# Delta rule of the RWKV-7 half: masked products and keys merged in their order of use, and one empty slot per tile left out

## The reference, cut to what matters

```python
def _rwkv7_scan(r, w, k, v, a, b, s0, reverse, emit):
    def step(s, inp):
        r_t, w_t, k_t, v_t, a_t, b_t = inp
        sa = jnp.einsum('bhvk,bhk->bhv', s, a_t)
        s = s * w_t[:, :, None, :] + sa[..., None] * b_t[:, :, None, :] + v_t[..., None] * k_t[:, :, None, :]
        y = jnp.einsum('bhvk,bhk->bhv', s, r_t) if emit else None
        return s, y
...
s_fin, ys = lax.scan(step, s0, xs, reverse=reverse)
...
y = ys[0] + ys[1]
mu = jnp.mean(y, axis=-1, keepdims=True)
var = jnp.mean(jnp.square(y - mu), axis=-1, keepdims=True)
yn = ((y - mu) * lax.rsqrt(var + RW_GN_EPS)).reshape(bsz, l, RW_WIDTH) * lnx_g + lnx_b
yn = yn + (bonus[0] + bonus[1]).reshape(bsz, l, RW_WIDTH)
```

## Time and profile before

| | us |
|---|---|
| median of 3 runs | 3844.43 (3835.66 to 3857.89) |
| profiled execution | 3846.75, its span 3844.9 |
| this stage, first load issued to last output normed | 772.90 to 1296.40, some 523 |
| PE busy over the span | 3337.7 (87%) |
| DVE, ACT, POOL busy over the span | 2382.1, 1908.6, 824.9 |

### The profile page before, as it was taken

One profiled execution on the slowest core, in us unless ns is written; L12 is line 12 of the kernel. 1 busy time (PEld: TensorE's weight loads), 2 busy tenths in 40 slices (PEclk: granted clock), 3 DMA queues, 4 the chain that ended last, 5 costly groups with the idle time before them and its releaser, 6 DMA issues. The chain is left out here.

```text
span 3844.9 us, 90156 instructions
## 1 busy us (share of the span) xinstructions
PE 3337.7 (87%) x33248; PEld 2259.3 (59%) x33248; DVE 2382.1 (62%) x4428; ACT 1908.6 (50%) x2994; POOL 824.9 (21%) x1095
## 2 busy tenths in 40 slices
PE   4899799768888697879989989999699999698699
PEld 0899798756666575633333333333377778576577
DVE  1688688845566575537767767777485753076631
ACT  0576567645555343217757767776423221066520
POOL 4000000045666200522212222221332323100000
PEclk6999899879999798989999999999999999898899
DMA  8354534432233337669799999950724223465352
GB/s 318 78 165 160 163 128 146 164 85 59 58 82 102 123 101 250 121 233 323 228 293 351 337 349 345 293 139 9 250 76 121 66 82 104 113 145 137 106 174 77
DMA packets 561734, 639.75 MB, mean 166 GB/s; under 512 B 108682, under 2 KB 472998, under 8 KB 558230
## 3 DMA queue, kind: packets, MB, share of 16 engines
q1 hardware_dynamic: 536038, 564.59, 46.2%
q0 software_dynamic: 25216, 69.34, 7.4%
q10 hardware_dynamic: 48, 0.05, 0.0%
HBM read 489.41 MB, written 161.74 MB: 169 GB/s over the span
## 5 line engine op out<-in xcount | busy, mean ns | idle before, releaser
L2626 PE MATMUL routed_p_gu<-routed_fixed,routed_x 128*32 128x512 f32 x3840 | 569.6, 597 | 0.0
L2626 PE MATMUL routed_p_gu<-moe_exp_w,routed_x 128*32 x1280 | 568.6, 597 | 0.7 <-DVE routed_fixed L2741 0.7
L2741 DVE COPY routed_fixed<-moe_exp_w 128x1024 f32 x640 | 400.5, 684 | 47.9 <-DMA moe_exp_w<-in_exp_w_up_dram 39.6
L2680 ACT COPY routed_fixed<-moe_exp_w 128x1024 f32 x320 | 332.7, 1047 | 148.2 <-PE routed_p_y L2641 78.1
L544 PE MATMUL front_ps<-front_a_high,front_w_high 128*128 128x320 f32 (+1 forms) x1120 | 363.3, 324 | 16.4 <-DVE front_w_low L797 13.5
L544 PE MATMUL front_ps<-front_a_high,front_w_low 128*128 128x320 f32 (+1 forms) x1120 | 354.4, 316 | 0.0
L544 PE MATMUL front_ps<-front_a_low,front_w_high 128*128 128x320 f32 (+1 forms) x1120 | 354.3, 316 | 0.0
L2626 PEld LDWEIGHTS routed_p_gu<-moe_exp_w,routed_x 128*32 128x32 f32 x1280 | 135.0, 110 | 353.8 <-issue 353.8
L2693 ACT COPY routed_fixed<-routed_wd 128x1024 f32 x240 | 235.3, 1043 | 127.2 <-PE routed_p_gu L2626 91.3
L3650 PE MATMUL pre_ps<-pre_a_high,pre_w_high 128*128 128x512 f32 x720 | 286.9, 399 | 13.2 <-ACT pre_xb L3811 6.6
L2641 PE MATMUL routed_p_y<-routed_wd,routed_hT 128*32 x640 | 289.1, 594 | 5.2 <-ACT routed_fixed L2693 5.2
(11 more groups left out here) (547 smaller groups left out, 7483.9 us busy)
## 6 DMA issues: line engine op xcount, KB each, us to landing
moe_exp_w<-in_exp_w_gate_dram SPq DMA_DIRECT2D x64, 1024.0 KB
moe_exp_w<-in_exp_w_up_dram SPq DMA_DIRECT2D x64, 1024.0 KB
routed_wd<-in_exp_w_down_dram SPq DMA_DIRECT2D x64, 1024.0 KB
front_wt<-in_w_in_dram SPq DMA_DIRECT2D x70, 512.0 KB, 4.4
mod_w<-in_w_mod_dram SPq DMA_DIRECT2D x24, 1024.0 KB, 18.2
pre_wt<-in_w_in_dram SPq DMA_DIRECT2D x44, 512.0 KB, 4.0
rw_abrk<-front_rb SPq DMA_DIRECT2D x64, 320.0 KB
rwmix_src<-rw_abrk SPq DMA_DIRECT2D x80, 192.0 KB, 2.5
```

The source lines that it names most:

```text
L2626: op = nc.tensor.matmul(p_gu[spot(s), :], x[:, b % 2, k, spot(s)], w, start=(k == 0), stop=(k == KD - 1))
L2680: nc.scalar.copy(fixed[:, place_of(b, c), 0, :], wgu[:, bass.ds(e % WS, 1), c * D:(c + 1) * D].rearrange("p o n -> p (o n)"))\
L2741: op = nc.vector.tensor_copy(fixed[:, place_of(b, c), s - 1, :], wgu[:, bass.ds(es[s] % WS, 1), c * D:(c + 1) * D].rearrange("p o n -> p ( ...
```

## The change

Three things are done at once. First, b leaves `src` and is loaded into a new tile `pair` in halves of 64 tokens, each beside the half of k that is used with it, so that a tile's b and k have one layout `[channel, d, step, token half]`: 14 DMAs per group and tile in place of 10. Second, the transposes of b and k write d = 0 into one bank and d = 1 into the other, in the layout of `bk`, and the products write their results by kind of product, not by chunk (`product_to`): each of the copies to `bk`, and each of the masks `at` and `bkT`, is then one instruction over 128 partitions in place of two over 64. Third, the slot `rest1` is left out of the list, so that `t0` stands two slots behind `prod`, and a tile has 23 slots (31 with the norm). `OFFSET` stays 6.

```diff
-    A, R, B, K, V = 0, 1, 2, 0, 1
+    A, R, V = 0, 1, 0
-        src, kv = each("src", [P, 2, 3, 2, P]), each("kv", [P, 2, 2, 2, P])
+        src, kv = each("src", [P, 2, 2, 2, P]), each("kv", [P, 2, 1, 2, P])
+        pair = each("pair", [P, 2, 2, 2, P])
-        LOADS = 10
+        LOADS = 14
-            out = ["turn", "lay", "rest0", "prod", "masked", "rest1", "t0"] + norm[0:1]
+            out = ["turn", "lay", "rest0", "prod", "masked", "t0"] + norm[0:1]
+        def product_to(b, rows, h, d, c, other):
+            first, last = 2 * other + d, 4 + 2 * c + d
+            return b[rows, h, :].rearrange("p (k t) -> p k t", t=HEAD)[:, slice(first, last + 1, last - first), :]
-                    sp.dma_start(src[u][:, z, :, d, :], rw["abrk"][d, 0:3, rows, tk].rearrange("j p t -> p j t"))\
+                    sp.dma_start(src[u][:, z, :, d, :], rw["abrk"][d, 0:2, rows, tk].rearrange("j p t -> p j t"))\
-                        sp.dma_start(kv[u][:, z, K, d, half(1 - c)], rw["k"][d, rows, tk]).then_inc(loaded[u][z], 16)
+                        at_step = chunk_of(c, d)
+                        sp.dma_start(pair[u][:, z, d, at_step, half(c)], rw["abrk"][d, 2, rows, tk]).then_inc(loaded[u][z], 16)
+                        sp.dma_start(pair[u][:, z, d, at_step, half(1 - c)], rw["k"][d, rows, tk]).then_inc(loaded[u][z], 16)
...
-                    for bank, first, rows in ((0, 0, x[:, B]), (0, 2 * P, kv[u][:, z, V]), (1, 0, kv[u][:, z, K])):
-                        for d in range(2):
-                            op = nc.tensor.transpose(b[:, bank, span(first + d * P, P)], rows[:, d], consts["ident"][:, :])
+                    for d in range(2):
+                        for s in range(2):
+                            nc.tensor.transpose(b[:, d, span(s * P, P)], pair[u][:, z, d, s], consts["ident"][:, :])
+                    for d in range(2):
+                        op = nc.tensor.transpose(b[:, 0, span(2 * P + d * P, P)], kv[u][:, z, V, d], consts["ident"][:, :])
...
-                    for side in range(2):
-                        op = nc.scalar.copy(stacked_rows(bk[u], side, side), turned_rows(b, 0, 0, side))
-                    op.then_inc(by_scalar[u], 1)
+                    nc.scalar.copy(bk[u][:, 0].rearrange("p s t -> p (s t)"), b[:, 0, span(0, 2 * P)]).then_inc(by_scalar[u], 1)
...
+                def product(k):
+                    return b[:, :, span(k * P, P)].rearrange("p h (e t) -> p h e t", e=2)
                 def strict(out, other):
-                    for c in range(2):
-                        rows = half(1 - c if other else c)
-                        op = nc.vector.tensor_tensor(out[u][rows].rearrange("p (e h) t -> p h e t", h=2), product(rows, c, 0),
-                                                     mask(MASK_AFTER)[rows].rearrange("p e h t -> p h e t"), ALU.mult)
-                    op.then_inc(by_vector[u], 1)
+                    nc.vector.tensor_tensor(out[u][:].rearrange("p (e h) t -> p h e t", h=2), product(other),
+                                            mask(MASK_AFTER).rearrange("p e h t -> p h e t"), ALU.mult).then_inc(by_vector[u], 1)
                 if p == "turn":
-                    for side in range(2):
-                        op = nc.vector.tensor_copy(stacked_rows(bk[u], side, 1 - side), turned_rows(b, 1, 0, side))
-                    op.then_inc(by_vector[u], 1)
+                    nc.vector.tensor_copy(bk[u][:, 1].rearrange("p s t -> p (s t)"), b[:, 1, span(0, 2 * P)]).then_inc(by_vector[u], 1)
```

More of the change, by code:

```diff
@@ L1196, in body @@
                             for h in range(2):
-                                to = span((2 * c + d) * P, P)
                                 queries = x[half(h), A:R + 1, d, half(c)]
-                                nc.tensor.matmul(b[half(c), h, to], x[half(h), B, d, half(c)], queries, start=True, stop=True)
-                                op = nc.tensor.matmul(b[half(1 - c), h, to], kv[u][half(h), z, K, d, half(1 - c)], queries,
+                                nc.tensor.matmul(product_to(b, half(c), h, d, c, 0), pair[u][half(h), z, d, chunk_of(c, d), half(c)], queries,
+                                                 start=True, stop=True)
+                                op = nc.tensor.matmul(product_to(b, half(1 - c), h, d, c, 1), pair[u][half(h), z, d, chunk_of(c, d), half(1 - c)], queries,
                                                       start=True, stop=True)
@@ L1349, in heads @@
                     return ap.rearrange("p h e v -> p (h e) v")
-                def product(rows, c, side):
-                    v = b[rows, :, span(2 * P * c, 2 * P)].rearrange("p h (e j t) -> p h e j t", e=2, j=2)
-                    return v[:, :, :, side, :]
+                def product(k):
+                    return b[:, :, span(k * P, P)].rearrange("p h (e t) -> p h e t", e=2)
                 def strict(out, other):
-                    for c in range(2):
-                        rows = half(1 - c if other else c)
-                        op = nc.vector.tensor_tensor(out[u][rows].rearrange("p (e h) t -> p h e t", h=2), product(rows, c, 0),
-                                                     mask(MASK_AFTER)[rows].rearrange("p e h t -> p h e t"), ALU.mult)
-                    op.then_inc(by_vector[u], 1)
+                    nc.vector.tensor_tensor(out[u][:].rearrange("p (e h) t -> p h e t", h=2), product(other),
+                                            mask(MASK_AFTER).rearrange("p e h t -> p h e t"), ALU.mult).then_inc(by_vector[u], 1)
                 if p == "turn":
                     PE.wait(dve, products[u], n, p)
-                    for side in range(2):
-                        op = nc.vector.tensor_copy(stacked_rows(bk[u], side, 1 - side), turned_rows(b, 1, 0, side))
-                    op.then_inc(by_vector[u], 1)
+                    nc.vector.tensor_copy(bk[u][:, 1].rearrange("p s t -> p (s t)"), b[:, 1, span(0, 2 * P)]).then_inc(by_vector[u], 1)
                 elif p == "prod":
@@ L1373, in body @@
                     for c in range(2):
-                        op = nc.vector.tensor_tensor(cc[u][:, c], product(slice(0, P), c, 1),
+                        op = nc.vector.tensor_tensor(cc[u][:, c], product(2 + c),
                                                      mask(MASK_FROM).rearrange("p e h t -> p h e t"), ALU.mult)
```

## The result

The change takes **3862.79 us** (median of 20 runs; one of them took 6703.07 and is left out of the ratio), the kernel before 3846.86 beside it: ratio **1.0033 [1.0024, 1.0042]**. That is slower, within the 0.5% that was forecast as no change, and 9 us over the 3854 predicted. The profiled execution took 3862.59.

The account below looks back on a forecast made before the run. The order of 24 steps was taken to bind, with no engine full. Plain tiles +12.6, normed tiles -5.1 and loads +1.7 make +9.2 on the profiled 3846.75, 3856; with the median 2.3 lower, 3854 us, range 3830 to 3878.

Parts of the forecast that it names:

- Loads: First tile: PE's first transpose stands behind fourteen DMA issues, not ten, +1.7 us; later loads stay ahead.
- Plain tiles: Tiles 0 to 6, without the norm: a period goes from 46.55 to 48.35 us, +1.8; seven of them +12.6.
- windows of 4.98: From a group's products to its `t0`: each window costs the DVE and POOL floor, 4.98 us; -3.2 per period.
- Gaps: From a group's `t0` to the next group's products: 7.4, 7.4, 9.1 and 4.5 us; +1.7 (first two), +2.7, +0.6.
- Third gap: Behind group 2's `t0`: S of group 0 waits for POOL's `faded`; 9.1 us for 6.40, +2.7; bounds 7.4 and 10.0.
- two waits of S per period: Sign in the changed profile: DVE's S waits for POOL's `faded` twice per period, 1.5 to 2 us.
- The merge's worth: Merging saves 1.27 us of DVE per group and tile, nearly all covered; one `at` piece lowers the window's floor to 4.98.
- DVE's relief reaches the path: Faster rival: 5.1 us of DVE work leave each period, plain period 43.8 us, total 3822; chance 0.12.
- Normed tiles: Three periods with the norm, 32 steps before: the whole left-out step is gained, -5.1 us; ends -5.1 and +5.4.
- The clock: Rival: more waiting on PE drops its clock to 1.2 GHz; one such period costs some 34 us, 3888; chance 0.04.

Follow-up runs that it names:

- the runs without the identity: POOL's identity addition on `TT` left out, in the change (ratio 0.9969) and in the change with slot `rest1` kept (0.9952); ratios to the kernel before.
- The merge alone: The change with slot `rest1` kept (24 steps), so merged instructions and new loads only; ratio 0.9960 to the kernel before.
- Masks later: The change with POOL's second and third X made one slot later, in the slot of `t0`; ratio 0.9993 to the kernel before.
- The run without the identity: The change with POOL's identity addition on `TT` left out; ratio 0.9969 to the kernel before.
- the best kernel: The change with `rest1` kept, `rest0` left out in tiles without the norm, both states' `faded` made early; ratio 0.9874 to the kernel before.
- other slot, state early: The change with `rest1` kept, `rest0` left out instead, and the first state's `faded` made in the slot of `t4`; ratio 0.9979 to the kernel before.

## Why the prediction held, and where its steps failed

- **Loads**: +1.7 forecast; +1.6 measured at PE's first transpose, +1.1 at the first products, counted from the first load. The first transpose (780.70) came 1.85 us behind the last of fourteen issues, 1.98 behind the last of ten before. The rule of the Trainium skill that transfers under 512 bytes don't reach line rate (DMA: Bandwidth & Descriptors, Specifications) shows no cost here: the eight loads into `pair` of the first tile landed 2.0 us behind their issue (median), where the four of k, with rows as short, took 2.2 before, and the two of `src` 2.2, where they took 2.4.

```profile
778.85 0.43 SPq L1145 DMA_DIRECT2D rwmix_kv<-rw_v  x1
...
780.70 1.12 PE L1197 MATMUL rwmix_ps<-ident,rwmix_pair 128*128 128x128 f32 x4 [31.21 <-DMA rwmix_kv<-rw_v]
```

- **Plain tiles**: +12.6 forecast, +13.0 measured, and the hit is in part luck. The working: windows of 4.98 hold in groups 1 to 3 and the runs without the identity show why; the windows' sum is 20.85 (forecast 19.9), since group 0's is 5.2 to 6.4. Gaps 7.14, 7.14, 8.5 to 9.2, 4.2 to 4.7 (forecast 7.4, 7.4, 9.1, 4.5) sum to 27.89, forecast 28.4. Where no low clock falls into them, the pieces are 5.18, three of 4.98, and 7.14, 7.14, 8.53, 4.24: a period of 47.2 and not 48.35. The gaps were forecast 1.35 us too long, and the clock, which had no term in the sum, made up for most of that.
- **Third gap**: two waits of S per period, as said, but of 3.0 us on the mean and not 1.5 to 2. The kernel before has two as well (13 in the same stretch, of 0.4 and 1.9 us in steady tiles), where the prediction read one; so their number was no sign of the change, their length was. The gap was priced at 1.7 us above the one with S on time (9.1 against 7.4); the runs put it at 0.9 (8.77 against 7.91) before S waits for PE instead. The rest of the 9.1 was PE's own chain.
- **The merge's worth** was put at one piece of `at` per window, 12 us of plain tiles. The merge alone gained 8.3 there and 6.6 in the normed tiles; beside the slot it is worth 29.7 (370.8 against 341.1). That fits the rival "DVE's relief reaches the path" for the merge; the slot took it back.
- **Normed tiles** are the step that failed, the term "I take the whole step, -5.1 us": -1.5 measured (+0.65, -1.57, -0.55 to the stage's end). The sum was 3.6 us short by this term. In tile 8 the windows lost 5.5 us together and the gaps gained 4.0, where none was taken for them; 1.8 of that is the last gap, 17.39 for 15.63 in tile 7, with the same work at a lower clock (by stretch, tile 7 and tile 8):

```profile
1164.00:1179.63 15.63, 12.74 (x375) 9.87 (x379) 8.32 (x26) 9.34 (x29) 9.24 (x18) 1.00 0.15 36
1215.46:1232.85 17.39, 14.97 (x374) 11.64 (x378) 8.26 (x26) 9.33 (x29) 9.26 (x18) 0.80 0.24 64
```

"Masks later" has the same order on PE and a clock of 1.00 in tiles 7 and 8, and is 3.8 us shorter there: 1.6 in group 0's window of tile 7 (5.18 for 6.78) and 2.0 in that last gap, while every other window and gap agrees within 0.3. So by this comparison most of what the term lacks is the clock, which it left out. The run without the identity is 7.3 us shorter in these two tiles, with windows 4.5 shorter than those of "masks later"; so POOL's row binds there as well.

- **The clock** was a rival at 0.04, priced for a whole period at the lower level. It came, but for some 4 us in each period (0.04 to 0.05 of 48 us are missing in the granted clock, and it has only a half to lose). Group 0's window in tiles 3 to 5 (the same work), and the time around its products in tile 5, by stretch:

```profile
931.11:936.28 5.17, 4.68 (x162) 3.96 (x158) 2.53 (x8) 3.04 (x10) 2.67 (x6) 1.00 0.03 6
978.75:985.14 6.39, 6.09 (x160) 5.14 (x158) 2.32 (x7) 2.83 (x9) 2.82 (x6) 0.76 0.02 4
1027.64:1033.80 6.16, 5.62 (x160) 4.90 (x158) 2.56 (x8) 3.01 (x9) 2.68 (x6) 0.84 0.01 3
...
1020.00:1026.00 6.00, 3.20 (x78) 2.38 (x77) 2.33 (x8) 2.95 (x9) 5.43 (x12) 1.00 0.32 74
1026.00:1029.60 3.60, 3.60 (x90) 3.48 (x91) 0.75 (x3) 1.48 (x4) 0.52 (x2) 0.53 0.05 12
1029.60:1036.00 6.40, 5.86 (x172) 4.67 (x165) 3.48 (x11) 2.65 (x8) 4.88 (x9) 1.00 0.16 40
```

PE was busy 3.20 of 6 us, waiting for POOL and for S; then the granted clock stood at about half, 1.2 GHz, and group 0's products, now PE's bound, took longer: the window is 5.2 in tiles 1 to 3 and 5.7 to 6.4 in tiles 4 to 6. The rule of the Trainium skill that the slow state is the default, which activity lifts (TensorE: Matmul & The Clock Gate, What's actually happening), agrees with these rows in its direction. From such pieces, with and without the low clock, an estimate of its price in the change: 2.8 us in these windows, 1.2 in the third gaps of tiles 1 and 2, 2.0 in the fourth gaps of tiles 3 to 6, so 6 of the 13 us of plain tiles, with tile 0 left out.

So the change comes out near no change because two effects nearly cancel: the merge gains 0.4%, and the slot, left out on the one side of the products where POOL's row needed its cover, loses 0.7%. How the slot's loss divides between the windows' floor and the clock is known by the estimate above alone, and why the clock falls where it does stays open. Whether the change's own slot would pay with the second `faded` early too wasn't tried; no wait for `faded` was left in that order.

## What to carry to other kernels

An empty slot in an interleaved order isn't empty: other groups' work runs there and covers a chain on other engines; before it is given up, the chain's length behind it is to be compared with the steps that remain (4.98 us against 3.9 here). Short work that another engine waits for goes ahead of long work that nobody needs yet on an in-order engine: two `faded` of 0.55 us, moved ahead of the masks, together with the normed tiles left at their 32 steps, turned the 23 steps of the plain tiles from no gain (0.9994) into 1.3%. And a cure counts only together with the order it is made in: the same move was worth nothing that can be told with 24 steps (0.9960 and 0.9956). A total that comes out as forecast doesn't show that its terms do: compare them one by one, and the granted clock of each.

## What the runs showed of the hardware that was not expected

A waiting PE can cost twice: where it was busy about half of 6 us, it ran the next 3.6 at a granted clock of 0.53, and each period of tiles 1 to 6 of the change has such a stretch (0.95 or 0.96 over the period). The total of its waits does not tell it: from 835 to 1110 us PE waited 39.5 us before, in 94 waits and at 1.00, and 41.3 in the change, in 61. Waits over 1 us go with the fall, 5 before, 15 in the change and none in the best kernel, but not always: "other slot, state early" has 13 and stays at 1.00. A DVE mask over 128 partitions took 414 ns (`bkT`) and 424 (`at`), one over 64 took 422, so the merge really is one instruction for the price of a half.
